# GpSimd takes tile 1's gain products in two norms and half of the band norm; decay exponentials move behind the first softmax

## The reference

```python
h = rms_norm(x, norm_mix); proj = h @ w_in            # first block, 5888 columns
att = sliding_window_attention(...)                   # softmax with sinks, ALiBi
ret = retention_chunkwise(rq, rk, rv)                 # decay tables exp(log_g * distance), 4 heads
merged = sigmoid(ga) * (att @ w_att_o) + sigmoid(gr) * (ret @ w_ret_o)
x = x + merged @ w_out
h = rms_norm(x, norm_ffn)                             # "norm2"
x = x + (silu(h @ w_gate) * (h @ w_up)) @ w_down
x = rms_norm(x, final_norm)
xn = rms_norm(x, ln_mix_g); proj = xn @ w_in_2        # "norm3", second block, 2560 columns
b_out = banded_chunk_attention(rms_norm(q, q_g), rms_norm(k, k_g), v, rel_bias)   # "band": 8 heads of 64, each normed
x = x + concat(gmlp(u, v), b_out) @ w_out_2
x = x + peer_ffn(rms_norm(x, ln_ffn_g), ...)          # per token and head 16 rows of a table of 16384 experts
```

## Time and profile before

| | before |
|---|---|
| median of 3 runs (lowest to highest) | 1173.13 us (1172.97 to 1173.32) |
| span of the profiled execution | 1171.0 us |
| PE busy | 1055.2 us (90%) |
| PEld busy | 658.3 us (56%) |
| DVE busy | 794.3 us (68%) |
| ACT busy | 613.2 us (52%) |
| POOL busy | 359.6 us (31%) |

### The profile page before, as it was taken

The page is one execution under the profiler, slowest core; times in us unless marked ns, Lnnn a source line. Parts: engine busy times, 40 slices in busy tenths (PEclk is TensorE's granted clock), DMA queues, the critical chain, the costliest instruction groups (busy, mean ns, idle before and its releaser), DMA issues.

```text
span 1171.0 us, 13207 instructions
## 1 busy us (share of the span) xinstructions
PE 1055.2 (90%) x3820; PEld 658.3 (56%) x3820; DVE 794.3 (68%) x1698; ACT 613.2 (52%) x1347; POOL 359.6 (31%) x283
## 2 busy tenths in 40 slices
PE   8999999999999999998999899877777777878777
PEld 7788888888888877885554444323222223323232
DVE  5763667765545588879686776776676667666755
ACT  7464564554445466836665555445444444444453
POOL 1000000100000000024455544555566566556542
PEclk9999999999999999999999999999999999999999
DMA  9463347955635754669999999999999999999997
GB/s 325 144 203 121 126 135 246 311 183 186 194 101 180 243 186 163 207 241 421 422 420 422 421 421 422 421 421 422 421 421 421 421 423 415 421 422 420 416 419 293
DMA packets 95760, 369.49 MB, mean 316 GB/s; under 512 B 6544, under 2 KB 30104, under 8 KB 63072
## 3 DMA queue, kind: packets, MB, share of 16 engines
q0 software_dynamic: 38464, 273.46, 56.5%
q1 hardware_dynamic: 57248, 95.45, 24.6%
HBM read 367.82 MB, written 1.06 MB: 315 GB/s over the span
## 4 chain that ended last, share of the span: by engine, by line
PE 48%; DMA 23%; DVE 8%; ACT 7%; issue 7%; POOL 5%; SPq 1%; POOLq 0%; ACTq 0%; DVEq 0%
DMA uv_ring<-in_peer_uv,expert 22%; PE gemm L1739 12%; PE gemm L1741 11%; PE gemm L1740 11%; PE gemm L2155 9%; POOL uv_ring L479 5%; DVE uv_ring L1625 2%; PE trb L1733 2%; ACT diag L937 1%; ACT L931 1%; ACT L903 1%; DVE w_both L979 1%; PE mmb L1821 1%; ACT wgt L934 1%; ACT hid_g L931 1%
## 5 line engine op out<-in xcount | busy, mean ns | idle before, releaser
L2155 PE MATMUL gemm<-uv_ring,diag 128*128 128x512 f32 x1020 | 493.9, 621 | 102.8 <-ACT diag L937 102.3
L479 POOL DMA_INDIRECT uv_ring<-in_peer_uv,expert x256 | 348.1, 1360 | 354.0 <-PE gemm L2155 193.6
L1625 DVE CUSTOM_DVE_ANT_0 uv_ring<-uv_ring,gains_xT 128x1024 f32<-128x1024 f32 x256 | 312.4, 1225 | 172.7 <-DMA uv_ring<-in_peer_uv,expert 172.5
L2155 PEld LDWEIGHTS gemm<-uv_ring,diag 128*128 128x128 f32 x1020 | 184.7, 194 | 385.0 <-ACT diag L937 224.2
L979 DVE TENSOR_TENSOR w_both<-raw,w_both 128x1024 fp32r<-128x1024 f32 (+1 forms) x184 | 192.9, 1061 | 146.5 <-ACT w_both L532 146.0
L532 ACT ACTIVATE w_both<-raw 128x1024 fp32r<-128x1024 f32 (+1 forms) x184 | 168.8, 929 | 176.1 <-PE gemm L1741 174.2
L1740 PE MATMUL gemm<-w_both,hT_hi 128*128 128x512 f32 (+1 forms) x592 | 227.5, 384 | 0.0
L931 ACT ACTIVATE hid_g<-hid,scales 128x1 f32<-128x1 f32 x256 | 75.0, 293 | 280.7 <-DVE hid L1625 279.8
L1739 PE MATMUL gemm<-w_both,hT_hi 128*128 128x512 f32 (+1 forms) x544 | 215.8, 397 | 4.6 <-DVE w_both L979 4.3
L1741 PE MATMUL gemm<-w_both,hT_lo 128*128 128x512 f32 (+1 forms) x544 | 208.9, 384 | 0.0
L1740 PEld LDWEIGHTS gemm<-w_both,hT_hi 128*128 128x128 f32 x592 | 111.6, 188 | 26.5 <-issue 7.0
(11 more groups left out here) (291 smaller groups left out, 897.4 us busy)
## 6 DMA issues: line engine op xcount, KB each, us to landing
raw<-in_w_in SPq DMA_DIRECT2D x30, 1024.0 KB, 5.1
raw<-in_w_gate SPq DMA_DIRECT2D x22, 512.0 KB, 4.0
raw<-in_w_up SPq DMA_DIRECT2D x22, 512.0 KB, 5.0
raw<-in_w_down SPq DMA_DIRECT2D x22, 512.0 KB, 3.3
raw<-in_w_out SPq DMA_DIRECT2D x8, 1024.0 KB, 5.1
uv_ring<-in_peer_uv,expert POOLq DMA_INDIRECT x258, 14.3
raw<-in_w_ret_o SPq DMA_DIRECT2D x4, 1024.0 KB, 5.4
raw<-in_peer_w_query SPq DMA_DIRECT2D x4, 1024.0 KB, 5.1
```

The costliest lines, as they stand in the source:

```text
L479: nc.gpsimd.indirect_dma_start(out=uv_ring[k % RING][:, 0:width], out_offset=None, in_=peer_uv, in_offset=bass.IndirectOffsetOnAxis(ap=exp ...
L1625: V.tensor_tensor_reduce(out=u_row, in0=u_row, in1=xn[:, b, :], scale=1.0, scalar=0.0, op0=ALU.mult, op1=ALU.add, accum_out=hid[par][:, k: ...
L2155: last = nc.tensor.matmul(gemm[2 * b + n][:], diag[k % 4][:], uv_ring[k % RING][:, D + n * CHUNK:D + (n + 1) * CHUNK], start=(begin and k ...
```

## The change

Four edits.

1. The twelve decay exponentials on ACT go from behind chunk 0's output to behind the second `softmax_exp` and the sinks, ahead of chunk 5's split.
2. In norm2 and norm3 tile 1's two `gained` products are done by POOL, each as soon as the sum that it reads is in `x_sb` (`g_free`). `normed` becomes one semaphore for each tile. In norm2 DVE's sum for tile 1 moves ahead of two quarters of its split. In norm3 DVE says on a new semaphore that `mix2_row` is made, and waits for POOL (`normed[1]`) before it scales tile 1 of `x_sb` in place. Norm 4 stays on DVE.
3. In the band norm POOL squares tile 1 (into a second buffer, `sq[1]`), while DVE squares and sums tile 0; DVE then sums both. After the Newton step each engine scales its tile.
4. POOL's load of `keys_t` stands behind its own scaling.

```diff
@@ GpSimd, behind the loads of the gain rows
-            pool.wait_ge(qk_normed, TB)
+            def gained(half, row, bank, count):
+                cols = slice(half * CHUNK, (half + 1) * CHUNK)
+                pool.wait_ge(g_free[bank], count)
+                nc.gpsimd.tensor_tensor(xn[:, 1, cols], x_sb[:, 1, cols], row[:, cols], ALU.mult).then_inc(normed[1], 1)
+
+            pool.wait_ge(ffn_landed, 16)
+            for half in range(2):
+                c = C_OUT + half
+                gained(half, ffn_row, 2 * (c % 2) + 1, c // 2 + 1)
+            pool.wait_ge(mix_row_ready, 1)
+            for half in range(2):
+                gained(half, mix2_row, 2 * half + 1, (C_IN2 - 2 + half) // 2 + 1)
+            for n in range(2):
+                pool.wait_ge(g_free[2 * n + 1], (C_IN2 + n) // 2 + 1)
+            qk = proj2[:, 1, D:2 * D]
+            nc.gpsimd.tensor_tensor(sq[1][:], qk, qk, ALU.mult).then_inc(squares_ready, 1)
+            pool.wait_ge(band_rstd_ready, 1)
+            qk = qk.rearrange("p (h d) -> p h d", d=HD)
+            nc.gpsimd.tensor_tensor(qk, qk, rstd[:, 16:32].unsqueeze(2).to_broadcast([P, 16, HD]), ALU.mult).then_inc(qk_normed[1], 1)
             pool.dma_start(keys_t[:], peer_keys_t).then_inc(keys_landed, 16)
@@ ScalarE, behind chunk 0's output
-            act.wait_ge(consts_made, 5)
-            for h in range(RH):
-                nc.scalar.activation(decay_q[:, h, :], q_pos[:], ACT.Exp, scale=log_decay[h])
-                nc.scalar.activation(decay_k[:, h:h + 1], k_age[:], ACT.Exp, scale=log_decay[h])
-                nc.scalar.activation(decay_t[:, h, :], age[:], ACT.Exp, scale=log_decay[h]).then_inc(decay_made, 1)
@@ ScalarE
             nc.scalar.activation(sink_e[:], sink_e[:], ACT.Exp).then_inc(exp_done, 1)
+            (the same five lines)
@@ VectorE, norm_behind
                 lo_columns(name, (0, 1))
-                dve.wait_ge(g_free[2 * (1 - c % 2) + 1], (c - 1) // 2 + 1)
+                residual(c, 1, (1,), scale)
                 lo_at(c + 1, quarters=(2, 3))
-                gained(1, 0, row)
-                residual(c, 1, (1,), scale)
-                dve.wait_ge(g_free[2 * (c % 2) + 1], c // 2 + 1)
-                gained(1, 1, row)
                 lo_columns(name, (2, 3))
@@ VectorE, down_in
-                for n in range(2):
-                    dve.wait_ge(g_free[2 * n + b], (C_IN2 - 2 + n) // 2 + 1)
-                    gained(b, n, mix2_row)
+                if b == 0:
+                    for n in range(2):
+                        dve.wait_ge(g_free[2 * n + b], (C_IN2 - 2 + n) // 2 + 1)
+                        gained(b, n, mix2_row)
@@ VectorE, band
-            for b in range(TB):
-                qk = proj2[:, b, D:2 * D]
-                me.link(V.tensor_tensor(sq[:], qk, qk, ALU.mult))
-                me.link(V.tensor_reduce(ss[:, 16 * b:16 * b + 16], sq[:].rearrange("p (h d) -> p h d", d=HD), axis=AX.X, op=ALU.add))
+            qk = proj2[:, 0, D:2 * D]
+            me.link(V.tensor_tensor(sq[0][:], qk, qk, ALU.mult))
+            me.link(V.tensor_reduce(ss[:, 0:16], sq[0][:].rearrange("p (h d) -> p h d", d=HD), axis=AX.X, op=ALU.add))
+            dve.wait_ge(squares_ready, 1)
+            me.link(V.tensor_reduce(ss[:, 16:32], sq[1][:].rearrange("p (h d) -> p h d", d=HD), axis=AX.X, op=ALU.add))
```

More of the change, by code:

```diff
@@ L251, in two_block_kernel @@
         var_ready, sd_ready = sem("var_ready"), sem("sd_ready")
-        normed = sem("normed")
+        normed, mix_row_ready = [sem("normed0"), sem("normed1")], sem("mix_row_ready")
+        squares_ready, band_rstd_ready = sem("squares_ready"), sem("band_rstd_ready")
         squared = sem("squared")
@@ L652, in _ @@
             nc.scalar.activation(sink_e[:], sink_e[:], ACT.Exp).then_inc(exp_done, 1)
+            act.wait_ge(consts_made, 5)
+            for h in range(RH):
+                nc.scalar.activation(decay_q[:, h, :], q_pos[:], ACT.Exp, scale=log_decay[h])
+                nc.scalar.activation(decay_k[:, h:h + 1], k_age[:], ACT.Exp, scale=log_decay[h])
+                nc.scalar.activation(decay_t[:, h, :], age[:], ACT.Exp, scale=log_decay[h]).then_inc(decay_made, 1)
             for c in (4, 5):
@@ L1041, in gained @@
                 cols = slice(half * CHUNK, (half + 1) * CHUNK)
-                V.tensor_tensor(xn[:, b, cols], x_sb[:, b, cols], row[:, cols], ALU.mult).then_inc(normed, 1)
+                V.tensor_tensor(xn[:, b, cols], x_sb[:, b, cols], row[:, cols], ALU.mult).then_inc(normed[b], 1)
             for q in range(4):
@@ L1790, in rows @@
                 def rows(n, half, b):
-                    pe.wait_ge(normed, 4 * NORM[name] + n + 1)
+                    pe.wait_ge(normed[b], 2 * NORM[name] + half + 1)
                     return xn[:, b, half * CHUNK:(half + 1) * CHUNK]
@@ L2039, in norm4_columns @@
             def norm4_columns(half, b):
-                pe.wait_ge(normed, 4 * NORM["norm4"] + 2 * b + half + 1)
+                pe.wait_ge(normed[b], 2 * NORM["norm4"] + half + 1)
                 turn(TR[f"norm4_{half}{b}"], [xn[:, b, half * CHUNK + i * P:half * CHUNK + (i + 1) * P] for i in range(4)])
```

19 lines of the change are left out of this document (11 added, 8 removed).

## The result

| | before | changed |
|---|---|---|
| median (lowest to highest) | 1173.05 us (1171.91 to 1174.45), 10 runs | 1176.13 us (1174.68 to 1178.99), 10 runs |
| span of the profiled execution | 1171.0 us | 1175.5 us |

A forecast was written before the change was run, and what follows sets the result against it. PE was taken to bound the front half, whose shift reaches the end one to one; 0.38 + 0 + 1.1 + 1.2 = +2.7 us on 1173.1 gave 1175.8 us, range 1172.3 to 1177.3 us.

The forecast's parts named there:

- The exponentials: Moved decay exponentials: 1.60 us gained at 27.73, 1.98 us lost before the turning of heads 2 and 3; sum +0.38 us.
- norm2: Tile 1's products on POOL in norm2: ready before PE's turn, so nothing, at most +0.65 us.
- norm3: Tile 1's products on POOL in norm3: PE begins quarter 2 later; +1.1 us, taken between two orders with hold-up.
- POOL's price: A 128x512 two-input product on POOL was taken at 1.25 us, twice the lower bound of 0.62 us.
- the orders named: In norm3: POOL, DVE's quarter, POOL costs +1.3 us; both POOL products back to back cost +0.8 us.
- The band norm: POOL's squares and scaling of tile 1 delay chunk 43's split, for which PE waits; +1.2 us.
- the middle between the orders: Band norm: POOL beginning first costs +1.8 us, DVE beginning first +0.6 us; the middle, +1.2 us, was taken.
- The prices from the page: Skill page's factor of 1.96 on DVE's times: 1.35 and 2.41 us a product, sum about 3.4 us, time 1176.5.
- POOL doesn't hold DVE up: Rival for norm3 and the band norm: no hold-up of DVE; sum -0.5 us, 1172.6 us; chance 0.22.
- The projection's gain stays: Rival at the turning of heads 2 and 3: 1.60 us kept, 1.98 hidden; sum 0.7 us, 1173.8 us; chance 0.06.
- Twice as slow: Rival on POOL's products in norm3 and the band norm: 2.5 and 4.3 us; sum 9.8 us, 1182.9 us; chance 0.05.
- The side: Outcome for the whole kernel: slower (above 1175.5 us) 0.48, same 0.46, faster (below 1170.8 us) 0.06.

The follow-up runs named there:

- decay_only: The kernel before with only the twelve exponentials moved behind the sinks; +1.5 us against before (ratio 1.0004 to 1.0022).
- pool_only_2: The kernel pool_only unchanged, another execution profiled; one run, front half +1.11 us against before.
- norm2_band: The changed kernel with the exponentials at their old place and norm3's products back on DVE; +0.1 us against before (ratio 0.9994 to 1.0012).
- norm3_wait: pool_only, with DVE splitting its two quarters in norm3 only after both POOL products are done; +2.2 us against before (ratio 1.0006 to 1.0024).
- decay_half: The kernel before with only the last six of the twelve exponentials moved behind the sinks; -0.6 us against before (ratio 0.9989 to 1.0007).
- pool_only: The changed kernel with the twelve exponentials back at their old place; +1.8 us against before (ratio 1.0004 to 1.0022).

## Why the prediction was right, and what in it was wrong

The forecast of +2.7 us is the front half's +2.75 us almost to the number, and the measured 1176.13 us lies 0.3 us above 1175.8, most of it the 0.25 us outside the span. But two of its terms are wrong by more than a microsecond, in opposite directions.

- **The exponentials, forecast +0.38 us.** The chain was read rightly: DVE's split, the copy and PE's wait of about 2 us for `ret_qk` stand where the prediction has them. Without the low clock the edit costs 0.05 to 0.17 us (three executions of decay_only); the gain at 28 is 2.0 us instead of 1.60, of which 0.2 is lost again by 59. What failed is the step that priced PE's wait by its length alone. In the changed kernel the low clock behind it adds 1.56 us, so the term is +1.69 us there. I had written the wait down and not asked what PE does behind it.
- **norm2, forecast 0.** Right: +0.0. POOL's second product stands still until DVE's quarter ends and DVE's two quarters take 3.44 us instead of 2.45, both in slack.
- **norm3, forecast +1.1 us.** Right: +1.09 us in the changed kernel, +1.11 in pool_only_2. Of the orders named, the first one came: POOL, quarter, POOL. POOL's price was right as well: 1.29 us for the first product where 1.25 were taken. The order was forecast at +1.3 us; the quarter between took 1.08 us in place of 1.18 and the second product 1.12, and that makes it +1.1. PE's wait stands ahead of the two turns (0.38 and 1.55 us), not at quarter 2, where the prediction looked for it.
- **The band norm, forecast +1.2 us.** Wrong: -0.03 us in the changed kernel's profile, and norm2_band shows -0.04 for norm2 and the band norm together. The step that failed is the price of POOL's product and the middle between the orders. A product of 128x1024 takes 1.75 us behind DVE's operation and not 2.14, twice on the path, which is 0.78 us less; and DVE began first (443.45 against 443.46), the order for which I had +0.6. It did so, by 0.01 to 0.02 us, in each of the eight executions with the band norm on POOL. 0.6 - 0.78 = -0.18 us; the wait at chunk 43 shrank from 0.96 to 0.84 us, -0.12.
- **The prices from the page.** The factor of 1.96 gave 1.35 and 2.41 us. Measured are 1.28 us for 128x512 and, behind a hold-up, 1.75 us for 128x1024, against DVE's 0.69 and 1.23 us. The Trainium skill's figure ("GPSIMD Engine Reference", section 3.1) is for rows of 2048 elements; the factor is near it at 512 (1.85) and lower at 1024 (1.4). Its advice (section 4.1), to leave such work to VectorE, holds here: POOL's share gained nothing in norm2 and the band norm and cost 1.1 us in norm3, where the hold-up adds to the slower operation.
- **The rivals.** "POOL doesn't hold DVE up" falls (2.93 against 1.22 us; norm3_wait). "The projection's gain stays" falls (decay_half: given back one to one). "Twice as slow" falls. The side was right: 1176.13 us lies above the 1175.5 us from which the prediction counted slower, by a narrow margin (the interval of the ratio begins at 1.0020).

Summed up as measured in the changed kernel's profile: 0.13 + 1.56 + 0 + 1.09 - 0.03 = 2.75 us. The forecast agrees because the cost that it lacked (1.56 us) is nearly what it had too much at the band norm (1.23 us) and in the trade of the exponentials (0.25 us). That the two sides cancel is luck. A right total says little of its terms.

What stays open: what decides whether the low clock comes (why the changed kernel had it at 75 us in both its profiles and decay_only in none of three, and why behind the queries it keeps to two programs); and why the median of decay_only (+1.5) stands more than a microsecond above the front half of its profiled executions (+0.05 to +0.17). Executions with a low stretch would give that; single runs of the time don't tell. Of norm3_wait's +2.2 us, +1.0 is its front half and 0.25 lies outside the span, and the interval takes in the sum of the two (it begins at +0.7 us).

## What to carry to other kernels

A wait that moves is not free even when its length is: before work is moved behind a chain, ask whether the chain has slack in front of the engine at its end (here PE, waiting for a copy), and look for a gap on the moved work's own engine instead; in ACT's own wait twelve exponentials kept 1.5 of the 2.0 us that they had freed. Handing a product with two inputs from DVE to POOL saves DVE nothing while DVE has two-input work of its own to do: each stands still for the other's whole instruction, and only what runs beside work with at most one input from SBUF (the sum at 444.71, the sums up to 418.23) is gained. And when a forecast comes true, measure its parts one by one before believing them.

## What the runs showed of the hardware

- PE's granted clock fell to its lower level right behind waits of 1.93 us (twice) and of 0.38 and 1.54 us (once), stayed there for 3 to 4 us although PE was busy again, and cost 1.5 to 1.6 us each time. Behind the same waits it stayed at 1.00 in three executions of decay_only, one of pool_only and, in norm3, in both of the changed kernel; behind the wait of 1.60 us at 28 us it did in five executions of five, and behind one of 0.95 us in one of one. The same program can go either way, on different chips. Behind a wait of 1.55 us that all fourteen executions have behind the queries, four (both of the changed kernel, both of pool_only) have a granted clock of 0.64 to 0.77 from 528 to 532 us; their second halves, 646.9 to 648.4 us, show no price for it.
- A product on POOL with both inputs in SBUF takes 1.27 to 1.29 us for 128x512 when nothing holds it up, against DVE's 0.69 us. Held up, it takes about 1.15 us from the end of DVE's operation, and one of 128x1024 takes 1.75 us, against DVE's 1.23 us; so about 0.1 us of an operation passes during the hold-up, and 128x1024 alone would take about 1.9 us (an estimate from these numbers).
- Each of the two engines stands still for the other's whole operation when both read two inputs from SBUF. A sum of DVE with one input (1.22 us, with POOL's squares beside it) and one whose second input lies in PSUM (1.28 us a pair, before and now, POOL's product beside it 1.29 us) neither hold POOL up nor are held up. A mask on POOL, with one input, is held up as well (2.17 us in place of 0.62, beside DVE's multiplication), and holds DVE up in turn (3.92 us in place of 3.49).
- An operation that must wait in this way counts as busy in the trace: DVE's 794 us hide what it lost.
